# Rope scores of the cached pages as two matmuls on a high-and-low stack, and two weight blocks of the next stage computed at the end of the page stage

## The chip, the cores and the metric

The kernel runs on one core of a Trainium2 chip. Its time is the device time of one execution in microseconds (us). A core has a tensor engine (PE, with its weight loads as PEld), a vector engine (DVE), a scalar engine (ACT), GpSimd (POOL), and a queue that issues most of the DMAs (SP). The engines run their own instruction streams and meet only at semaphores.

## The reference

One layer of a hybrid decoder serves a prompt of 256 tokens and 8 sample sequences of 4 new tokens each (288 token columns in all, T below). Per layer:

```
xn = RMSNorm(x)
h  = x + W_out( sig(g_A) * W_A(mLSTM(xn)) + sig(g_B) * W_B(MLA(xn)) )
y  = h + ConvFFN(RMSNorm(h))
```

The change lies in the MLA branch of the sample sequences. Each has 1024 past positions in 8 pages of 128, chosen by a page table; a page holds 512 latent columns and 64 rotary (rope) columns per position. For each of 16 heads:

```
k      = qk_norm(concat(latent @ w_uk, k_rope))          # 128 + 64 columns
scores = (q . k) * ATTN_SCALE                            # also against the 4 new tokens, masked
p      = softmax(scores)
o      = (p @ latent) @ w_uv
```

The norm of a key is one number for each position and head, so a score is (latent part + rope part) divided by a root. The mLSTM branch takes q, k, v and output gates of 8 heads from one projection of xn.

## The kernel before

All large products are made in a form of float32 called fp32r, for which an operand is split into a high part and the rest: `h*w = hH*wH + hL*wH + hH*wL`, three matmuls that each take one pass. A plain fp32 matmul needs no split; the trace writes it as two records. A transpose is a matmul against `ident`.

The stages follow each other with a barrier between them (`recycle()`):

1. **The queries and prompt attention.** Norm of x; the small projections; queries and keys of 16 heads in a loop `for h in range(BH + 3)`, in which PE makes `keys(h)`, turns chunks of w_uk (`flip`), and makes the absorbed queries (q times w_uk) of the samples. `qrS` is the rope part of the sample queries, 64 x 16 heads x 32 tokens.
2. **The page stage.** For 8 sample sequences (`batch`), 8 pages each: `turn(b, j+1)` transposes the next page (4 transposes of latent columns into PSUM bank 4, one of the 64 rope columns into bank 7), ACT copies the high part into `latH` (`hi`) and DVE subtracts for `latL` (`lo`); then `keys(b, j)` makes 5 groups of columns for the key norms, and in group 0 64 more columns, the scores (16 heads x 4 tokens), by 12 fp32r matmuls a group. The rope part of the scores is one fp32 matmul ahead of them in group 0: `rT` (64 x 128, the page's rope turned) by `qrC` (64 x 64), line 1521. ACT squares the groups (`squares`), DVE sums them (`sums`). The softmax and values of sequence b-1 are spread over the pages of b. Batches 0, 1, 6 and 7 are written out, 2 to 5 are a loop.
3. **The end of the page stage.** For the last sequence nothing is left to put beside: scale, maxima, exps, `values`, `last_denominators`, `turn_out` (line 1606), 128 small matmuls by w_uv (line 1650), four transposes (line 1656), and the store of the result to DRAM (`hb_dram[:, :, S_P:]`). ACT and DVE then split the first weight block (`split_hi`, `split_lo` of `At(N0)`). SP has meanwhile brought back xnH and xnL from DRAM (semaphore `xn_back`); their place in SBUF, and that of the split weights, is that of w_uk in the page stage.
4. **The head stage.** 8 mLSTM heads, 6 weight blocks each. `block(n)` is 48 matmuls: 16 chunks by xnH and xnL with the high weights, then 16 with the low ones. ACT makes `split_hi(n+1)`, DVE `split_lo(n+1)` during block n, in two buffers; SP keeps four 1 MB weight loads in the buffers `stage`. N0 is 9, so the first two blocks of head 0 are At(N0) and At(N0 + 1).
5. Branch and output projections and the FFN, in the same blocks. The branch stage reads back the attention output `hb`.

PE runs in order. Nothing plans the order at run time: it is the order of the text, and a semaphore wait holds back all that is behind it on its engine.

## Time and profile before

| | us |
|---|---|
| median of 3 runs | 2946.97 (2946.59 to 2951.3) |
| the profiled execution's own time | 2953.18 |
| its span, first to last instruction | 2951.4 |
| PE busy (share) | 2896.2 (98%) |
| DVE busy | 1429.4 (48%) |
| ACT busy | 1138.8 (39%) |
| mean granted PE clock | 0.991 |

Busy times overlap between engines. A PE matmul's duration holds its latency, so matmuls that follow each other without a gap overlap in the records; what one costs is the distance from its start to the next one's start. The granted clock is 1.00 at 2.4 GHz and 0.50 at 1.2 GHz.

### The profile page before, as it was taken

How to read it: one execution, taken by the hardware profiler on the slowest of the kernel's cores; microseconds unless marked ns; L12 is line 12 of the kernel's file. 1: busy time of each engine (PE TensorE's matmuls, PEld its weight loads, DVE VectorE, ACT ScalarE, POOL GpSimd, SP SyncE). 2: the span in 40 equal slices, each digit the busy share in tenths (PEclk: the TensorE clock that was granted, in tenths of full speed). 3: DMA queues.
4: the chain of work that ended last, by engine and by line, in shares of the span. 5: the costliest groups of instructions: out<-in, count | busy, mean ns of one | idle time of the engine just before them, and what ended most of it. 6: DMA issues, size and time to landing. Idle time of an engine off the chain costs nothing. (4 is left out here: it accounts for less than half of the span.)

```text
span 2951.4 us, 49867 instructions
## 1 busy us (share of the span) xinstructions
PE 2896.2 (98%) x19398; PEld 2699.2 (91%) x19398; DVE 1429.4 (48%) x2174; ACT 1138.8 (39%) x1875; POOL 104.9 (4%) x346
## 2 busy tenths in 40 slices
PE   8998999999999998999999999999999999999999
PEld 7865898888898896899999999999999999999999
DVE  4465433333333332355555434445667654667644
ACT  5535332332332231344444333334444433444433
POOL 0100000000000000000000000002100000000100
PEclk9998999999999998999999999999999999999999
DMA  6522301001001102756565655556555556555464
GB/s 204 208 80 88 106 1 33 17 17 33 29 5 33 33 1 93 208 157 197 171 186 173 189 171 160 167 151 199 165 163 164 162 148 175 172 170 161 145 180 129
DMA packets 620546, 372.13 MB, mean 126 GB/s; under 512 B 23928, under 2 KB 602050, under 8 KB 619336
## 3 DMA queue, kind: packets, MB, share of 16 engines
q1 hardware_dynamic: 608200, 357.63, 40.6%
q10 hardware_dynamic: 11824, 11.50, 1.1%
q8 instruction: 112, 1.84, 0.2%
q0 software_dynamic: 368, 0.81, 0.1%
q14 instruction: 42, 0.34, 0.0%
HBM read 347.16 MB, written 22.75 MB: 125 GB/s over the span
## 5 line engine op out<-in xcount | busy, mean ns | idle before, releaser
L287 DVE TENSOR_TENSOR w_lo_b<-stage,w_hi_b 128x2048 fp32r<-128x2048 f32 (+1 forms) x289 | 619.2, 2143 | 425.0 <-ACT w_hi_b L280 424.9
L299 PE MATMUL bank<-xnH,w_hi_b 128*128 128x288 f32 x2784 | 756.2, 299 | 6.3 <-PEq L191 6.3
L300 PE MATMUL bank<-xnL,w_hi_b 128*128 128x288 f32 x2784 | 750.9, 296 | 0.0
L280 ACT ACTIVATE w_hi_b<-stage 128x2048 fp32r<-128x2048 f32 (+1 forms) x289 | 517.9, 1792 | 572.4 <-PE bank L304 536.8
L299 PEld LDWEIGHTS bank<-xnH,w_hi_b 128*128 128x128 f32 x2784 | 524.5, 188 | 15.9 <-issue 15.3
L300 PEld LDWEIGHTS bank<-xnL,w_hi_b 128*128 128x128 f32 x2784 | 524.2, 188 | 0.3
L1524 PE MATMUL bank<-ukH,latH 128*128 128x384 f32 (+2 forms) x1280 | 458.0, 358 | 0.0
L1526 PE MATMUL bank<-ukH,latL 128*128 128x384 f32 (+2 forms) x1280 | 452.4, 353 | 0.0
L1525 PE MATMUL bank<-ukL,latH 128*128 128x384 f32 (+2 forms) x1280 | 452.0, 353 | 0.0
L1755 DVE TENSOR_REDUCE rk<-sq_n 128x3 f32<-128x384 f32 (+1 forms) x320 | 184.9, 580 | 508.3 <-ACT sq_n L1679 508.3
L304 PE MATMUL bank<-xnH,w_lo_b 128*128 128x288 f32 x2784 | 396.6, 295 | 0.0
L304 PEld LDWEIGHTS bank<-xnH,w_lo_b 128*128 128x128 f32 x2784 | 378.2, 188 | 0.0
L1679 ACT ACTIVATE sq_n<-bank 128x384 f32<-128x384 f32 (+1 forms) x320 | 163.9, 512 | 443.1 <-PE bank L1526 443.1
L299 PE MATMUL bank<-haH,w_hi_b 128*128 128x288 f32 x1024 | 278.1, 299 | 6.8 <-PEq L191 3.9
L300 PE MATMUL bank<-haL,w_hi_b 128*128 128x288 f32 x1024 | 276.7, 297 | 0.0
L1524 PEld LDWEIGHTS bank<-ukH,latH 128*128 128x128 f32 x1280 | 240.9, 188 | 16.9
L1526 PEld LDWEIGHTS bank<-ukH,latL 128*128 128x128 f32 x1280 | 240.8, 188 | 14.4
L1525 PEld LDWEIGHTS bank<-ukL,latH 128*128 128x128 f32 x1280 | 240.9, 188 | 13.0
L299 PEld LDWEIGHTS bank<-haH,w_hi_b 128*128 128x128 f32 x1024 | 194.1, 190 | 7.5 <-issue 7.3
L300 PEld LDWEIGHTS bank<-haL,w_hi_b 128*128 128x128 f32 x1024 | 194.9, 190 | 0.0
L304 PE MATMUL bank<-haH,w_lo_b 128*128 128x288 f32 x1024 | 151.9, 295 | 0.0
L304 PEld LDWEIGHTS bank<-haH,w_lo_b 128*128 128x128 f32 x1024 | 141.5, 188 | 0.0
(471 smaller groups left out, 2786.1 us busy)
## 6 DMA issues: line engine op xcount, KB each, us to landing
stage<-in_w_in_dram SPq DMA_DIRECT2D x88, 1024.0 KB, 5.0
stage<-in_w_up_dram SPq DMA_DIRECT2D x88, 1024.0 KB, 5.3
stage<-in_w_down_dram SPq DMA_DIRECT2D x64, 704.0 KB, 4.5
latf<-in_cache_kv_latent_dram SPq DMA_DIRECT2D x64, 256.0 KB, 2.5
stage<-in_w_branch_a_dram SPq DMA_DIRECT2D x16, 1024.0 KB, 5.6
stage<-in_w_branch_b_dram SPq DMA_DIRECT2D x16, 1024.0 KB, 5.4
stage<-in_w_out_dram SPq DMA_DIRECT2D x16, 1024.0 KB, 5.6
stage<-in_w_uk_dram SPq DMA_DIRECT2D x8, 1024.0 KB, 5.0
```

What stands on the lines that cost most here:

```text
L280: act.activation(h, a, ACT.Copy).then_inc(w_hi, 1)
L287: dve.tensor_tensor(lo, a, h.bitcast(F32), ALU.subtract).then_inc(w_lo, 1)
L299: pe.matmul(out, hi, xH(k), start=first and k == 0, stop=False)
L300: pe.matmul(out, hi, xL(k), start=False, stop=False)
L304: mm = pe.matmul(out, lo, xH(k), start=False, stop=last and k == kc - 1)
L1524: pe.matmul(out, h, ukH[:, k, cols], start=g > 0 and k == 0, stop=False, skip_group_check=g == 0)
L1525: pe.matmul(out, h, ukL[:, k, cols], start=False, stop=False, skip_group_check=g == 0)
L1526: mm = pe.matmul(out, lo, ukH[:, k, cols], start=False, stop=k == LC - 1, skip_group_check=g == 0)
L1679: act.activation(sq[:, (j + g) % 2, 0:(h1 - h0) * NOPE], part, ACT.Square).then_inc(n_sq, 1)
L1755: dve.tensor_reduce(rk[:, b.mod(2), j, h0:h1], sq[:, (j + g) % 2, 0:(h1 - h0) * NOPE].rearrange("p (h d) -> p h d", d=NOPE), AX.X, ALU.add ...
```

## The change

**Rope part.** The first stage makes from `qrS` two stacks of 128 rows: `qHH` (the high part twice) and `qLZ` (the low part over zeros). For that PE multiplies `qrS` by the identity twice, into the two halves of bank 7 (at h = 5), ACT copies and DVE subtracts (at h = 6), and PE waits for it at h = 7. In the page stage `turn` transposes the page's last 128 columns once more, so that the rope lands on partitions 64 to 127 as well; ACT copies twice, and DVE subtracts the second copy: `rS` holds the high part over the low part. The fp32 matmul goes, and two fp32r matmuls of 64 columns with `rS` as stationary operand come behind the first matmul of group 0. `turn` and `keys` wait for DVE's subtraction (`f_rl`) where they waited for ACT's copy (`f_rt`). The rope of the new tokens (`krrT`) is changed alike. DVE's copy into `qrC` goes.

**Two blocks.** Blocks N0 and N0 + 1 move from the start of the head stage into the end of the page stage: N0 ahead of the last `turn_out`, N0 + 1 ahead of the last four transposes. Their splits move with them, and block N0 + 2 gets its `split_hi` at the end of the stage. The w_uv products go to banks 4 and 7 in place of 0 and 1, the transposes to banks 0 and 3 in place of 2 and 3.

**Placement.** The sample part of the attention output has a DRAM tensor of its own, and `hs` lies in `olat`'s place; the head stage waits for its store before it uses that place again. The branch stage reads `hb` with two DMAs.

```
                 sp.wait_ge(e_oev, 2 * p + 2)
-                sp.dma_start(hb_dram[:, 2 * p:2 * p + 2, 0:S_P], ho[:, p % 2]).then_inc(e_st[p % 2], 16)
+                sp.dma_start(hb_dram[:, 2 * p:2 * p + 2, :], ho[:, p % 2]).then_inc(e_st[p % 2], 16)
...
                     pe.wait_ge(ct_ev, 3)
+                    for a in range(2):
+                        mm = pe.matmul(bank[7][a * ROPE:(a + 1) * ROPE, :], ident[0:ROPE, 0:ROPE],
+                                       qrS[:].rearrange("p h (b s) -> p b h s", b=NB), start=True, stop=True)
+                    mm.then_inc(qd_mm, 1)
+                if h == 7:
+                    pe.wait_ge(qd_lo, 1)
...
                     latent_rows(2)
+                if h == 6:
+                    act.wait_ge(qd_mm, 1)
+                    act.activation(qHH[:].rearrange("p b q -> p (b q)"), bank[7][:], ACT.Copy).then_inc(qd_hi, 1)
...
                     dve.wait_ge(r_ss, 1)
+                if h == 6:
+                    dve.wait_ge(qd_z, 1)
+                    dve.wait_ge(qd_hi, 1)
+                    dve.tensor_tensor(qLZ[0:ROPE].rearrange("p b q -> p (b q)"), bank[7][0:ROPE, :],
+                                      qHH[0:ROPE].rearrange("p b q -> p (b q)").bitcast(F32), ALU.subtract).then_inc(qd_lo, 1)
...
                 need(pe, f_lo, b.of(NPG, j))
-                need(pe, f_rt, b.of(NPG, j))
+                need(pe, f_rl, b.of(NPG, j))
...
                     pe.transpose(bank[4][:, k * P:(k + 1) * P], latf[:, b.mod(2), j, k * P:(k + 1) * P], ident)
+                pe.transpose(bank[7][:, P:2 * P], latf[:, b.mod(2), j, KVL - ROPE:], ident)
...
                 pe.wait_ge(f_lo, b.of(NPG, j + 1))
-                pe.wait_ge(f_rt, b.of(NPG, j + 1))
+                pe.wait_ge(f_rl, b.of(NPG, j + 1))
...
                     out = key_bank(g)[:, 0:c1 - c0]
-                    if g == 0:
-                        pe.matmul(out[:, parts(s)[0]], rT[:, a, :], qrC[:, s, :], start=True, stop=False, skip_group_check=True)
...
                         h, lo = latH[:, a, k * P:(k + 1) * P], latL[:, a, k * P:(k + 1) * P]
-                        pe.matmul(out, h, ukH[:, k, cols], start=g > 0 and k == 0, stop=False, skip_group_check=g == 0)
-                        pe.matmul(out, h, ukL[:, k, cols], start=False, stop=False, skip_group_check=g == 0)
-                        mm = pe.matmul(out, lo, ukH[:, k, cols], start=False, stop=k == LC - 1, skip_group_check=g == 0)
+                        pe.matmul(out, h, ukH[:, k, cols], start=k == 0, stop=False)
+                        if g == 0 and k == 0:
+                            pe.matmul(out[:, parts(s)[0]], rS[:, a, :], qHH[:, bass.ds(b.of(), 1), :], start=False, stop=False)
+                            pe.matmul(out[:, parts(s)[0]], rS[:, a, :], qLZ[:, bass.ds(b.of(), 1), :], start=False, stop=False)
+                        pe.matmul(out, h, ukL[:, k, cols], start=False, stop=False)
+                        mm = pe.matmul(out, lo, ukH[:, k, cols], start=False, stop=k == LC - 1)
...
                     pe.matmul(ps, cnL[:, k, :], qh_, start=False, stop=False)
-                pe.matmul(ps, krrT[:], qrS[:].rearrange("p h (b s) -> p b h s", b=NB), start=False, stop=True).then_inc(f_sn, 1)
+                pe.matmul(ps, krrS[:], qHH[:].rearrange("p b q -> p (b q)"), start=False, stop=False)
+                pe.matmul(ps, krrS[:], qLZ[:].rearrange("p b q -> p (b q)"), start=False, stop=True).then_inc(f_sn, 1)
...
             last_denominators(At(NB - 1))
+
+            def first_block(n):
+                block(pe, At(n), At(n), lambda k: xnH[:, k, :], lambda k: xnL[:, k, :])
+            pe.wait_ge(xn_back, 32)
+            first_block(N0)
...
             pe.wait_ge(uv_in, 16 * LC)
-            pe.wait_ge(n_sq, KG * NPG * NB)
...
                     for g in range(4):
-                        mm = pe.matmul(bank[j // 2][g * N_S:(g + 1) * N_S, j % 2 * P:(j % 2 + 1) * P], olat[:, k, 4 * j + g, :],
+                        mm = pe.matmul(bank[(4, 7)[j // 2]][g * N_S:(g + 1) * N_S, j % 2 * P:(j % 2 + 1) * P], olat[:, k, 4 * j + g, :],
...
                 mm.then_inc(f_uv, 1)
+            first_block(N0 + 1)
...
                 for j in range(2):
-                    tr = pe.transpose(bank[2 + i][:, j * P:(j + 1) * P], ol[:, (2 * i + j) * P:(2 * i + j + 1) * P], ident)
+                    tr = pe.transpose(bank[3 * i][:, j * P:(j + 1) * P], ol[:, (2 * i + j) * P:(2 * i + j + 1) * P], ident)
...
                 act.activation(latH[:, j % 2, :], bank[4][:], ACT.Copy).then_inc(f_hi, 1)
-                act.activation(rT[:, j % 2, :], bank[7][0:ROPE, 0:P], ACT.Copy).then_inc(f_rt, 1)
+                act.activation(rS[0:ROPE, j % 2, :], bank[7][0:ROPE, 0:P], ACT.Copy)
+                act.activation(rS[ROPE:, j % 2, :], bank[7][ROPE:, P:2 * P], ACT.Copy).then_inc(f_rt, 1)
...
             exps(At(NB - 1))
+            split_hi(act, At(N0))
+            split_hi(act, At(N0 + 1))
             act.wait_ge(f_uv, 4)
-            act.activation(ol[:, 2 * P:], bank[1][:, 0:2 * P], ACT.Copy).then_inc(f_hq2, 1)
+            act.activation(ol[:, 2 * P:], bank[7][:, 0:2 * P], ACT.Copy).then_inc(f_hq2, 1)
...
                 act.wait_ge(f_h, i + 1)
-                act.activation(hs[:, 8 * i:8 * i + 8, :].rearrange("p h s -> p (h s)"), bank[2 + i][:, 0:2 * P], ACT.Copy).then_inc(f_hev, 1)
-            split_hi(act, At(N0))
+                act.activation(hs[:, 8 * i:8 * i + 8, :].rearrange("p h s -> p (h s)"), bank[3 * i][:, 0:2 * P], ACT.Copy).then_inc(f_hev, 1)
+            split_hi(act, At(N0 + 2))
...
         def _(dve):
-            dve.memset(krrT[:], 0.0).then_inc(f_zero, 1)
+            dve.memset(krrS[:].bitcast(F32), 0.0).then_inc(f_zero, 1)
...
             dve.wait_ge(f_zero, 2)
+            dve.wait_ge(f_kh, 1)
+            low = krrS[ROPE:, 0:N_S]
+            dve.tensor_tensor(low, bank[6][ROPE:, 0:N_S], low.bitcast(F32), ALU.subtract).then_inc(f_neg, 1)
...
                 dve.tensor_tensor(latL[:, j % 2, :], bank[4][:], latH[:, j % 2, :].bitcast(F32), ALU.subtract).then_inc(f_lo, 1)
+                dve.wait_ge(f_rt, b.of(NPG, j + 1))
+                low = rS[ROPE:, j % 2, :]
+                dve.tensor_tensor(low, bank[7][ROPE:, P:2 * P], low.bitcast(F32), ALU.subtract).then_inc(f_rl, 1)
...
                 s = b.mod(2)
-                dve.tensor_copy(qrC[:, s, :].rearrange("p (h q) -> p h q", q=S_S), qrS[:, :, bass.ds(b.of(S_S), S_S)])
...
             total(At(NB - 1))
+            split_lo(dve, At(N0))
+            split_lo(dve, At(N0 + 1))
...
             dve.wait_ge(f_uv, 2)
-            dve.tensor_copy(ol[:, 0:2 * P], bank[0][:, 0:2 * P]).then_inc(f_hq, 1)
-            split_lo(dve, At(N0))
+            dve.tensor_copy(ol[:, 0:2 * P], bank[4][:, 0:2 * P]).then_inc(f_hq, 1)
...
                 for j in range(steps(h)):
-                    if blocks:
+                    if blocks and not (h.i is None and h.c == 0 and j < 2):
...
                     act.activation(dws[:], bank[5][:, 0:DVE_], ACT.Copy, scale=gws[:, bass.ds(h.of(), 1)]).then_inc(H["ds"], 1)
+                    if h.i is None and h.c == 0:
+                        act.wait_ge(e_st[0], 16 * (BH // 4 + 1))
...
                     if blocks:
-                        split_hi(act, n + (j + 1))
+                        if not (h.i is None and h.c == 0 and j < 2):
+                            split_hi(act, n + (j + 1))
...
                     if blocks:
-                        split_lo(dve, n + (j + 1))
+                        if not (h.i is None and h.c == 0 and j < 1):
+                            split_lo(dve, n + (j + 1))
...
             sp.wait_ge(e_st[s], 16 * (BH // 4 + 1 - s))
-        sp.dma_start(hb[:], hb_dram).then_inc(hb_in, 16)
+        sp.dma_start(hb[:, :, 0:S_P], hb_dram).then_inc(hb_in, 16)
+        sp.dma_start(hb[:, :, S_P:], hbs_dram).then_inc(hb_in, 16)
```

What stands on PE around the rope of one page, before (names: `cst` holds the identity, `krr` is the tensor in which `qrC` lies):

```order
L1526 MATMUL bank<-ukH,latL 128x512
L1498 ISA
L86 REGISTER_ALU
L1502 MATMUL bank<-cst,latf 128x128 x4
L1503 MATMUL bank<-cst,latf 64x128
L86 REGISTER_ALU
L1521 MATMUL bank<-krr,rT 128x64
L1524 MATMUL bank<-ukH,latH 128x448
L1525 MATMUL bank<-ukL,latH 128x448
```

and at a page of the changed kernel:

```order
L1568 MATMUL bank<-cst,mxw 128x64
L86 REGISTER_ALU
L1521 MATMUL bank<-cst,latf 128x128 x4
L1522 MATMUL bank<-cst,latf 128x128
L1523 MATMUL bank<-cst,latf 64x128
L86 REGISTER_ALU
L1542 MATMUL bank<-ukH,latH 128x448
L1544 MATMUL bank<-qHH,rS 128x64
L1545 MATMUL bank<-qLZ,rS 128x64
L1546 MATMUL bank<-ukL,latH 128x448
```

A fifth full transpose comes in, and the rope matmul is replaced by two behind the first of the group.

What stands on PE at the end of the page stage, before:

```order
L1557 MATMUL bank5<-cst,psums 64x1
L1558 MATMUL bank5<-cst,psums 64x1
L1606 MATMUL bank6<-cst,ol_3086 128x64 x4
L1650 MATMUL bank0<-stage,olat 32x128 x32
L1650 MATMUL bank1<-latf,olat 32x128 x32
L1656 MATMUL bank2<-cst,ol_3086 128x128 x2
L1656 MATMUL bank3<-cst,ol_3086 128x128 x2
L1446 UNCONDITIONAL_BRANCH
L2037 UNCONDITIONAL_BRANCH
L299 MATMUL bank1<-xnH,w_hi_b 128x288
```

and in the changed kernel, where block N0 begins:

```order
L1579 MATMUL bank5<-cst,psums 64x1
L1580 MATMUL bank5<-cst,psums 64x1
L300 MATMUL bank1<-xnH,w_hi_b 128x288
L301 MATMUL bank1<-xnL,w_hi_b 128x288
L300 MATMUL bank1<-xnH,w_hi_b 128x288
L301 MATMUL bank1<-xnL,w_hi_b 128x288
L300 MATMUL bank1<-xnH,w_hi_b 128x288
L301 MATMUL bank1<-xnL,w_hi_b 128x288
```

The first block stands ahead of `turn_out`, where in the kernel before two branches (the barrier) lay between.

DVE at the same place, before:

```order
L1799 TENSOR_REDUCE psums<-sc_s 128x64
L1801 TENSOR_TENSOR psums<-psums,sc_s 32x64
L1805 RECIPROCAL rs<-bank5 128x1
L1812 TENSOR_SCALAR ol_3086<-bank6,rs 128x512
L1817 COPY olat<-bank6 128x16x4 x4
L1935 COPY ol_3086<-bank0 128x256
L287 TENSOR_TENSOR w_lo_b<-stage,w_hi_b 128x2048
```

and after:

```order
L1834 TENSOR_REDUCE psums<-sc_s 128x64
L1836 TENSOR_TENSOR psums<-psums,sc_s 32x64
L288 TENSOR_TENSOR w_lo_b<-stage,w_hi_b 128x2048 x2
L1840 RECIPROCAL rs<-bank5 128x1
L1847 TENSOR_SCALAR ol_3096<-bank6,rs 128x512
L1852 COPY olat<-bank6 128x16x4 x4
L1972 COPY ol_3096<-bank4 128x256
```

Two splits stand ahead of the reciprocal; the one at the end is gone.

## Rows read from the trace of the kernel before

**Rows 1.** The page: busy us (share of the span) and instructions.

```profile
PE 2896.2 (98%) x19398; PEld 2699.2 (91%) x19398; DVE 1429.4 (48%) x2174; ACT 1138.8 (39%) x1875; POOL 104.9 (4%) x346
```

**Rows 2.** Busy time by stretch: engines, granted PE clock, DMA share, GB/s.

```profile
1155.00:1188.30 33.30, 17.54 (x166) 10.39 (x165) 10.77 (x24) 6.23 (x11) 0.00 (x0) 0.72 0.55 202
```

**Rows 3.** Timeline of PE at one page: start us, us, instruction, count.

```profile
1086.46 0.60 PE L1502 MATMUL bank<-cst,latf 128*128 128x128 f32 x4
1086.89 0.27 PE L1503 MATMUL bank<-cst,latf 128*64 128x128 f32 x1
1087.09 0.43 PE L1521 MATMUL bank<-krr,rT 64*128 64x64 f32 x2
1087.45 0.47 PE L1524 MATMUL bank<-ukH,latH 128*128 128x448 f32 x1
1087.76 0.36 PE L1525 MATMUL bank<-ukL,latH 128*128 128x448 f32 x1
1087.97 0.36 PE L1526 MATMUL bank<-ukH,latL 128*128 128x448 f32 x1
```

**Rows 4.** Timeline of PE: eight records with full weights and 64 columns.

```profile
1142.11 1.00 PE L1606 MATMUL bank<-cst,ol 128*128 128x64 f32 x8
1143.04 0.43 PE L1521 MATMUL bank<-krr,rT 64*128 64x64 f32 x2
```

**Rows 5.** Timeline of ACT at a page: the copy of the turned rope.

```profile
563.70 0.26 ACT L1666 ACTIVATE rT<-bank 64x128 f32<-64x128 f32 x1
```

**Rows 6.** Timeline of PE in the key loop of the first stage.

```profile
168.36 0.62 PE L745 MATMUL bank<-u_reg,xT_reg 128*32 128x512 f32 x2
169.35 0.66 PE L734 MATMUL bank<-cst,stage 128*128 128x128 f32 x4
201.03 0.65 PE L734 MATMUL bank<-cst,stage 128*128 128x128 f32 x4 [1.27 <-DVE u_reg L1249]
```

**Rows 7.** Timeline of PE at the first two `turn`s; idle before in brackets.

```profile
293.28 1.12 PE L1502 MATMUL bank<-cst,latf 128*128 128x128 f32 x4 [2.31 <-DMA latf<-in_cache_k_rope_dram]
296.26 1.11 PE L1502 MATMUL bank<-cst,latf 128*128 128x128 f32 x4 [1.65 <-DVE latL L1750]
```

**Rows 8.** Timeline of PE from the last denominators into the head stage.

```profile
1172.71 1.63 PE L1606 MATMUL bank<-cst,ol 128*128 128x64 f32 x8 [1.12 <-DVE ol L1812]
1175.14 3.64 PE L1650 MATMUL bank<-stage,olat 128*32 128x128 f32 x64 [0.80 <-DVE olat L1817]
1181.09 1.01 PE L1656 MATMUL bank<-cst,ol 128*128 128x128 f32 x4
1188.34 0.58 PE L299 MATMUL bank<-xnH,w_hi_b 128*128 128x288 f32 x1 [6.25 <-PEq L191]
```

**Rows 9.** Timeline of ACT and DVE in the same stretch.

```profile
1163.54 0.24 ACT L1689 ACTIVATE sc_s<-sc_s 32x64 f32<-32x64 f32 x1
1182.41 1.90 ACT L280 ACTIVATE w_hi_b<-stage 128x2048 fp32r<-128x2048 f32 x1
1184.34 2.29 DVE L287 TENSOR_TENSOR w_lo_b<-stage,w_hi_b 128x2048 fp32r<-128x2048 f32 x1 [5.08 <-ACT w_hi_b L280]
```

**Rows 10.** Busy time by stretch there (columns as in rows 2).

```profile
1167.00:1170.00 3.00, 3.00 (x10) 0.71 (x6) 0.00 (x0) 0.00 (x0) 0.00 (x0) 0.55 0.26 111
1170.00:1172.00 2.00, 1.59 (x8) 0.38 (x6) 0.27 (x2) 0.00 (x0) 0.00 (x0) 1.00 0.00 0
1178.00:1180.00 2.00, 2.00 (x45) 2.00 (x41) 0.43 (x1) 0.00 (x0) 0.00 (x0) 0.51 0.04 8
1180.00:1182.00 2.00, 1.87 (x48) 1.29 (x39) 0.00 (x0) 0.73 (x2) 0.00 (x0) 1.00 0.00 0
```

**Rows 11.** The page: DMA issues, KB each, median us to landing.

```profile
stage<-in_w_in_dram SPq DMA_DIRECT2D x88, 1024.0 KB, 5.0
```

**Rows 12.** Timeline of PE: start of the third weight block, and ten matmuls on.

```profile
1203.56 0.29 PE L299 MATMUL bank<-xnH,w_hi_b 128*128 128x288 f32 x1
1204.88 0.30 PE L299 MATMUL bank<-xnH,w_hi_b 128*128 128x288 f32 x1
```

More of the change, by code:

```diff
@@ L198, in build @@
     xT_dram = nc.dram_tensor("xT_scratch", (P, KC, T), F32, kind="Internal").ap()
-    hb_dram = nc.dram_tensor("hb_scratch", (P, BH, T), F32, kind="Internal").ap()
+    hb_dram = nc.dram_tensor("hb_scratch", (P, BH, S_P), F32, kind="Internal").ap()
+    hbs_dram = nc.dram_tensor("hbs_scratch", (P, BH, N_S), F32, kind="Internal").ap()
     xnH_dram = nc.dram_tensor("xnH_scratch", (P, KC, T), F32, kind="Internal").ap()
@@ L313, in build @@
         c_new = sb(kept, "c_new", [N_S, KVL])
-        qrS = sb(kept, "qrS", [ROPE, BH, N_S])
+        qHH = sb(kept, "qHH", [P, NB, BH * S_S], F32R)
+        qLZ = sb(kept, "qLZ", [P, NB, BH * S_S], F32R)
         qlat = sb(kept, "qlat", [P, LC, NB, 2, BH, S_S], F32R)
@@ L424, in build @@
             u_reg = arena("u_reg", [P, 2, 2, KVL], 2 * XB + WB)
+            qrS = arena("qrS", [ROPE, BH, N_S], 2 * XB + WB + 8192)
             smr = arena("smr", [P, BH, N_S], 2 * XB + WB + 10240)
@@ L492, in build @@
             v_mm, v_ev = sem("vv_mm"), sem("vv_ev")
+            qd_mm, qd_z, qd_hi, qd_lo = (sem("qd_" + x) for x in ("mm", "z", "hi", "lo"))
             e_s, e_sc, e_sm, e_mx, e_ex, e_rc, e_nm, e_t, e_tev, e_o, e_oev = (
@@ L1141, in _ @@
                     dve.memset(cnL[:].bitcast(F32), 0.0).then_inc(cn_z, 1)
+                    dve.memset(qLZ[:].rearrange("p b q -> p (b q)").bitcast(F32), 0.0).then_inc(qd_z, 1)
                     dve.wait_ge(x_rt, 1)
@@ L1368, in build @@
             sq = sb(ph, "sq_n", [P, 2, GC])
-            qrC = krr2[0:ROPE, 0:2, 1, :]
-            rT = sb(ph, "rT", [ROPE, 2, P])
+            rS = sb(ph, "rS", [P, 2, P], F32R)
+            mxp = sb(ph, "mxp", [P, 2, P])
+            mxw = sb(ph, "mxw", [HQ, 2, P])
             sqr = sb(ph, "sqr_n", [P, 2, ROPE])
@@ L1379, in build @@
             sc = sb(ph, "sc_s", [P, 2, NJ, HQ])
-            mxp = sb(ph, "mxp", [P, 2, P])
             mxc = sb(ph, "mxc", [HQ, 2])
-            mxw = sb(ph, "mxw", [HQ, 2, P])
             psums = sb(ph, "psums", [P, 2, HQ])
@@ L1386, in build @@
             olat = sb(ph, "olat", [P, LC, BH, N_S])
-            hs = sc[:].rearrange("p a j q -> p (a j q)")[:, 0:BH * N_S].rearrange("p (h s) -> p h s", h=BH)
-            krrT = sb(ph, "krrT", [ROPE, P])
+            hs = olat[:].rearrange("p k h s -> p (k h s)")[:, 800:800 + BH * N_S].rearrange("p (h s) -> p h s", h=BH)
+            krrS = sb(ph, "krrS", [P, P], F32R)
             gb = sb(ph, "gb", [P, 2 * AH])
@@ L1409, in build @@
             n_k, n_sq, n_red = (sem("n_" + x) for x in ("k", "sq", "red"))
+            f_kh, f_rl = sem("f_kh"), sem("f_rl")
             (f_kt, f_fold, f_neg, f_zero, f_sn, f_sn1, f_scn, f_t, f_hi, f_rt, f_lo, f_ra, f_rr, f_rc, f_sev, f_snc, f_m8, f_mxp,
@@ L1491, in _ @@
                     sp.wait_ge(f_hev, 2)
-                    sp.dma_start(hb_dram[:, :, S_P:], hs).then_inc(e_st[0], 16)
+                    sp.dma_start(hbs_dram, hs).then_inc(e_st[0], 16)
                 @blk.tensor
@@ L1629, in batch @@
                                 gates(j)
-                    pe.transpose(bank[6][0:ROPE, 0:N_S], krr[0:N_S, 2, :], ident[0:N_S, 0:N_S]).then_inc(f_kt, 1)
+                    pe.transpose(bank[6][:, 0:N_S], krr2[0:N_S, 2].rearrange("p a e -> p (a e)"), ident[0:N_S, 0:N_S]).then_inc(f_kt, 1)
                     pe.wait_ge(f_neg, 1)
@@ L1721, in _ @@
                     act.wait_ge(f_zero, 2)
-                    act.activation(krrT[:, 0:N_S], bank[6][0:ROPE, 0:N_S], ACT.Copy).then_inc(f_neg, 1)
+                    act.activation(krrS[:, 0:N_S], bank[6][:, 0:N_S], ACT.Copy).then_inc(f_kh, 1)
                     for g in range(4):
@@ L2379, in _ @@
                         if j == i:
-                            act.wait_ge(hb_in, 16)
+                            act.wait_ge(hb_in, 32)
                             act.activation(hbH[:, q0:q1, :], hb[:, q0:q1, :], ACT.Copy).then_inc(hb_h, 1)
```

## Prediction, made blind

> **What bounds the kernel now.** I read the page first: PE is busy for 98% of the span [rows 1], so time is won only where PE does less, or where it stands still or runs at the lower clock. The table by stretch shows where that is: from the end of the last page to the head stage PE is busy for 17.54 us of 33.3, at a mean granted clock of 0.72 [rows 2]. The page stage itself is dense. The timeline gives the cost of one page's rope [rows 3], and the timeline of PE, ACT and DVE at the end of the stage gives the chain there [rows 8, 9]. Durations come from the profiled execution, 2953.18 us, 6.21 above the median of 2946.97; I work out a difference and take it from the median.
>
> **The page loop.** From the first transpose to the second large matmul a page takes 1087.76 - 1086.46 = 1.30 us [rows 3]: 0.43 for four transposes (0.107 each), 0.20 for the narrow one (0.107 and the time until the next matmul may begin), 0.36 for the two records of the fp32 rope matmul, 0.31 for the first large matmul, whose weight load nothing hides; the next takes 0.21. The change takes out the 0.36. It adds one transpose, 0.107. The narrow transpose is still the last, so its 0.20 and the 0.31 stay.
>
> The two fp32r matmuls of 64 columns load full weights each, and no record before has just this form. The nearest is `turn_out`: eight records with 128 x 128 weights and 64 columns take 1143.04 - 1142.11 = 0.93 us, 0.116 each [rows 4]; they are fp32, but a record of 64 columns streams for far less, so the weight load sets the distance. I take this: 0.23 for the pair. The cheap end is the stream alone: a matmul of 448 columns takes 0.21 [rows 3], so 64 columns take 0.03, 0.06 the pair. The dear end is the record of the rope matmul itself, 0.18 [rows 3], with a weight load of 0.11 laid bare behind them: 0.47. So a page goes from 1.30 to 0.54 + 0.20 + 0.31 + 0.23 = 1.28; 64 pages give 1.3 us. By the ends it would be 12 us gained (0.36 - 0.107 - 0.06 = 0.19 a page) or 14 us lost (0.22 a page).
>
> The Trainium skill ("TensorE: Matmul & The Clock Gate", section "LDWEIGHTS (loading the stationary operand)") gives columns / 1.2 ns for a weight load, so 107 ns for 128; the 0.116 above agrees. The same page, section "Back-to-back issue gap", puts a matmul of up to 64 columns at about 25 ns where nothing else holds it; by that alone the pair would cost 0.05 us, and the kernel would end where the second rival has it.
>
> ACT makes one more copy a page, 0.26 us [rows 5], and DVE a subtraction of 64 x 128, which I put at as much. Both stand behind `hi` and `lo` of the next page, more than 10 us ahead of its use, on engines that are busy for 39 and 48% [rows 1]; queued behind them are the squares and sums of group 0, whose PSUM bank PE wants back only a page later. Cost: nothing; without that cover it would be 0.5 us a page. Only at the first two pages does PE wait for this chain: the second `turn` waited 1.65 us for `latL` [rows 7], and now waits for the rope's subtraction behind it, +0.25 us. The new tokens' rope gets a DVE step ahead of their scores, 0.3 us; they are followed by a wait of 2.31 us for the page's DMA [rows 7], which hides it.
>
> **The first stage.** PE gets two fp32 matmuls of 64 x 64 weights and 512 columns into two halves of a bank. The nearest are the four column-tiled ones of line 745, which run side by side: from 168.36 to 169.35, 0.99 us for all four [rows 6]. The halves do not share columns of the array either, so I take 1.0; two in turn would be 2.0; the low end is 0, since PE later stands for 1.27 us for DVE [rows 6] and might only get there later. PE's wait at h = 7 I put at nothing: two key products and two sets of transposes lie between the multiplication and it, against one ACT copy and one DVE subtraction. Both are queued ahead of copies that PE waits for two steps later; if they slip, it is by the 0.7 us or so of a DVE operation of 512 columns, within the ends. DVE's zeroing of `qLZ` lies in the wait for x at the start.
>
> **The end of the page stage.** Before: PE is done with the denominators at 1172.71 - 1.12 = 1171.59, waits, `turn_out` at 1172.71, 0.80 of waiting, w_uv from 1175.14, transposes at 1181.09, and then nothing for 6.25 us, since ACT and DVE split block N0 until 1184.34 + 2.29 = 1186.63 before the barrier; PE resumes at 1188.34, 1.7 later [rows 8, 9]. The third block begins at 1203.56. Block length: ten matmuls take 1.32, so 48 take 6.3 [rows 12]; the first two took 15.2, 2.6 more than 12.6, because the clock had fallen.
>
> After, step by step:
> - Operands of block N0 are there: ACT is free at 1163.78, its two splits (1.90 each) end at 1167.6, DVE's (2.29 each) at 1170.4; xnH and xnL have landed when DMA falls still before 1170 [rows 9, 10]. Slack of DVE 1.2 us: its reciprocal is behind the splits.
> - Block N0 from 1171.6 to 1177.9. The clock had risen from 0.55 to 1.00 by 1170, after PE had been busy for some 6 us, and was at 0.51 again by 1178 [rows 10]; now PE does not pause behind 1171.6.
> - `turn_out` 0.93 [rows 4] to 1178.8; wait for `olat` 0.8 [rows 8], 1179.6.
> - w_uv: at clock 0.51 45 matmuls took 2.00 us; at 1.00 44 took 1.09 (1180.00 to 1181.09, the other 4 of the 48 being the transposes) [rows 8, 10]. 128 by 0.025 are 3.2, to 1182.8, where before they took 5.95.
> - Block N0 + 1 to 1189.1. From the first transpose to the end of ACT's copies took 1182.41 - 1181.09 = 1.3 [rows 8, 9]: 1190.4. SP's two weight loads start behind w_uv, at 1182.8; at 5.0 us [rows 11] the first is there by 1188.
> - `split_hi` of N0 + 2, 1.9: 1192.3; the barrier 1.7: block N0 + 2 begins at 1194.0. DVE's `split_lo` follows at once (its memsets and 2.3 us, about 3.5) and is wanted after 32 matmuls, over 4 us on.
>
> 1203.56 - 1194.0 = 9.5 us earlier, but an idle time of about 4 us lets the clock fall as the 6.25 did before, so block N0 + 2 pays the 2.6. Gain 6.9 us. What was late before, two splits and a barrier, is now one high split and the barrier; the next in line, loads of blocks N0 + 4 and on, have two blocks (12 us) from their issue against 5.0 each.
>
> The store and reload of `hb` I put at nothing: both are issued by SP, and the reload's first user is ACT two blocks later, 12.6 us. If the short pieces of the sample part held up the loads behind it on the queue by more than the three blocks that are loaded ahead, PE would stand; at worst a few us.
>
> **Sum.** -6.9 - 1.3 + 1.0 + 0.25 = -6.9 us: 2953.2 becomes 2946.3 in a profile, the median 2946.97 becomes 2940.1. A measurement of this kernel tells 0.2% (5.9 us) from no change, so the forecast is faster by slightly more than that.
>
> **Rivals.**
> 1. *The clock falls in the middle of the end stage.* For it: before, w_uv ran at 0.51 until 1180 although PE had stood for only 1.12 and 0.80 us since it was last at 1.00 [rows 8, 10]. Against: a dense block of 6.3 us now precedes. Price: w_uv back to 5.95 (+2.8) and a further 2.6 in block N0 + 1, 5.4 in all: 2945.5.
> 2. *The small matmuls hide their weight loads.* The pair at 0.06: 0.17 a page better, 10.9 us: 2929.2. Against it speak the 0.116 of rows 4, though those are fp32.
> 3. *The other side: the pair stalls the large matmuls.* Both add into columns that the matmul just ahead is still writing, and the large one behind finds its weights not loaded: 0.47 for the pair, 0.24 a page more than taken, 15.4 us: 2955.5. It makes the kernel no faster from a pair cost of 0.23 + 6.9 / 64 = 0.34, and slower by 0.2% from 0.43. For it: every change of shape in rows 3 costs 0.1. Against: `rS` is a full 128 x 128 operand, as are its neighbours.
> 4. *The moved blocks do not fill the gap.* If ACT's or DVE's splits or the reload of xn come after 1171.6 by several us, `turn_out` is held behind block N0 and the gap only moves: 2947, no change. The slack of 1.2 us speaks against it.
>
> **How the numbers follow.** Forecast 0.53, rivals in order 0.17, 0.12, 0.08, 0.10. The forecast's own spread, 2936 to 2943, comes from the first stage's 0 to 2 us, a tenth of a microsecond a page more or less in part, and the run-to-run spread of before. Faster than 2941.1: rival 2, and 0.65 of the forecast: 0.46. Slower than 2952.9: rival 3 and a rest: 0.09. The same: 0.45. The range leaves out the far part of rivals 2 and 3: 2931 to 2948.
>
> **What the profile after would show.** A page's stretch from first transpose to the second large matmul (L1546) at 1.28 us, L1544 to L1546 0.23 apart; PE idle of about 4 us, no more 6.25, ahead of the third block; w_uv in 3 to 4 us; clock 1.00 from 1170 to about 1190; the last stretch from the last denominators to block N0 + 2 of 22 us where it was 32. The forecast is wrong if the pair is not near 0.23, if block N0 has a wait ahead of it, or if the head stage runs dry of weights.

## The result, and the profile after

The changed kernel takes 2929.63 us (median of 4 runs, 2927.95 to 2931.32) against 2947.57 (4 runs) for the kernel before, measured beside it: ratio 0.9936, 95% interval [0.9924, 0.9947], 17.9 us less. The forecast was 2940.1, the range 2931 to 2948; the time lies below it. The profiled execution took 2930.21 us with a span of 2928.4, so in the profiles the difference is 23.0 us of span.

One execution of the kernel before beside e1 to e4 (7029.46 us) and one of e3 (5666.08 us) were slow, and the medians below leave them out.

The page of the kernel after answers to [rows 1] with less PE time (21.4 us less) from slightly more instructions:

```profile
PE 2874.8 (98%) x19466; PEld 2696.7 (92%) x19466; DVE 1453.3 (50%) x2233; ACT 1157.6 (40%) x1940; POOL 108.2 (4%) x346
```

The timeline of PE at a plain page after (start us, us, instruction, count), beside [rows 3]:

```profile
1036.83 0.60 PE L1521 MATMUL bank<-cst,latf 128*128 128x128 f32 x4
1037.27 0.27 PE L1522 MATMUL bank<-cst,latf 128*128 128x128 f32 x1
1037.37 0.27 PE L1523 MATMUL bank<-cst,latf 128*64 128x128 f32 x1
1037.40 0.45 PE L1542 MATMUL bank<-ukH,latH 128*128 128x448 f32 x1
1037.69 0.19 PE L1544 MATMUL bank<-qHH,rS 128*128 128x64 f32 x1
1037.71 0.28 PE L1545 MATMUL bank<-qLZ,rS 128*128 128x64 f32 x1
1037.83 0.45 PE L1546 MATMUL bank<-ukL,latH 128*128 128x448 f32 x1
1038.11 0.36 PE L1547 MATMUL bank<-ukH,latL 128*128 128x448 f32 x1
```

From the first transpose to the third large matmul this is 1038.11 - 1036.83 = 1.28 us; in [rows 3] it is 1087.97 - 1086.46 = 1.51. 64 pages by 0.23 are 14.7. The page loop, from its first large matmul to the end of its last, took 857.0 us before (298.13 to 1155.17) and 843.2 after (298.79 to 1141.95): 13.9 less, where the forecast had 1.3.

The timeline of PE from the last denominators into the head stage after (in brackets: idle before, and what ended it), beside [rows 8]:

```profile
1156.96 0.40 PE L300 MATMUL bank<-xnH,w_hi_b 128*128 128x288 f32 x1
1165.22 1.96 PE L1676 MATMUL bank<-stage,olat 128*32 128x128 f32 x64 [0.80 <-DVE olat L1852]
...
1179.45 0.37 PE L300 MATMUL bank<-xnH,w_hi_b 128*128 128x288 f32 x1 [3.50 <-PEq L191]
```

Block N0 begins right behind the denominators, at 1156.96, block N0 + 2 at 1179.45, 22.5 us later. The busy time by stretch (duration, PE, PEld, DVE, ACT, POOL busy, granted PE clock, DMA share, GB/s), a stretch of 33.3 us from just ahead of block N0, against 17.54 us busy at 0.72 in [rows 2]:

```profile
1155.00:1188.30 33.30, 29.00 (x312) 26.91 (x309) 9.08 (x15) 6.06 (x10) 0.63 (x1) 1.00 0.43 134
```

The 23.0 us of span by stretch: up to the first large matmul +0.7; the page loop -13.9; from its end to the end of the third weight block -10.8 (55.0 before, 44.1 after); the rest +1.0. In that rest ACT waits 4.41 us for a weight load (until 1191.09), and PE's fifth block begins 7.1 us behind its fourth, where 6.4 is usual: 0.7 us in which the head stage did run dry of weights, once.

### The profile page after: what moved, and what is told of

Read it like the earlier page. It is cut to its first block and busy times, and to the rows that moved or that the text cites. A ratio compares the mean times of both kernels' runs of the same rounds, so it can differ in the third digit from the quotient of the medians.

```text
span 2928.4 us, 50135 instructions
## 1 busy us (share of the span) xinstructions
PE 2874.8 (98%) x19466; PEld 2696.7 (92%) x19466; DVE 1453.3 (50%) x2233; ACT 1157.6 (40%) x1940; POOL 108.2 (4%) x346
## 5 line engine op out<-in xcount | busy, mean ns | idle before, releaser
L300 PEld LDWEIGHTS bank<-xnH,w_hi_b 128*128 128x128 f32 x2784 | 523.0, 188 | 14.2 <-issue 12.8
L1546 PE MATMUL bank<-ukL,latH 128*128 128x384 f32 (+2 forms) x1280 | 458.0, 358 | 0.0
L1542 PEld LDWEIGHTS bank<-ukH,latH 128*128 128x128 f32 x1280 | 241.2, 188 | 12.8
L1546 PEld LDWEIGHTS bank<-ukL,latH 128*128 128x128 f32 x1280 | 241.0, 188 | 12.4
```

Source lines behind the costliest of these rows:

```text
L300: pe.matmul(out, hi, xH(k), start=first and k == 0, stop=False)
L1542: pe.matmul(out, h, ukH[:, k, cols], start=k == 0, stop=False)
L1546: pe.matmul(out, h, ukL[:, k, cols], start=False, stop=False)
```

## Experiments

Theory A, formed from the traces of before and after: the 0.20 us behind the narrow transpose [rows 3] was not that transpose's. It was a wait of the weight load behind it, because the rope matmul's weights have 64 rows and its neighbours' 128. Rival B: the plain fp32 type of the rope matmul made it. Rival C: the narrow transpose made it, and in the changed kernel something hides it. The timelines of PE's weight loads, before:

```profile
1086.78 0.11 PEld L1503 LDWEIGHTS bank<-cst,latf 128*64 128x64 f32 x1
1087.09 0.29 PEld L1521 LDWEIGHTS bank<-krr,rT 64*128 64x128 f32 x2 [0.20 <-issue]
1087.45 0.19 PEld L1524 LDWEIGHTS bank<-ukH,latH 128*128 128x128 f32 x1
```

and after:

```profile
1037.27 0.11 PEld L1523 LDWEIGHTS bank<-cst,latf 128*64 128x64 f32 x1
1037.38 0.19 PEld L1542 LDWEIGHTS bank<-ukH,latH 128*128 128x128 f32 x1
1037.49 0.19 PEld L1544 LDWEIGHTS bank<-qHH,rS 128*128 128x128 f32 x1
```

Behind the narrow transpose's load the next one stood 0.31 us away before, and 0.11 after. Beside e1 to e4 the kernel before took 2948.63 us, beside e5 to e8 2946.84, and beside e9 to e12 2947.09; each ratio is against the one beside it.

**e1: the rope part alone.** The changed kernel with both blocks, their splits and the split of N0 + 2 back in the head turn:

```
-                    pe.wait_ge(xn_back, 32)
-                    first_block(N0)
...
-                    first_block(N0 + 1)
...
-                            if blocks and not (h.i is None and h.c == 0 and j < 2):
+                            if blocks:
```

> The changed kernel with its two weight blocks put back at the start of the head stage; rope stack and placement stay. Theory A (the 64-row fp32 matmul made PE wait 0.20 us a page for its own weight load, and that wait went with it): the page loop keeps its whole gain of 13.9 us, the start costs 0.7, so 13 us faster than before (ratio about 0.9955). Rival (the page gain depended on the blocks, or was one profile's chance): 3 us or less, as I predicted at first.

Measured: 2937.53 us against 2948.63, ratio 0.9963 [0.995, 0.9976], 11.1 us less. Its page loop takes 842.7 us, close to the 843.2 after.

**e2: the blocks alone.** The kernel before with both blocks moved as in the change.

> The kernel before with only the two weight blocks moved into the end of the page stage. Theory: the end stage gives 7 to 10 us in a profile: 6.9 by the shorter chain, 2.6 more if the clock stays at 1.00 through the idle time of 3.5 us ahead of block N0 + 2. Against the median of before, whose profile was a slow one at this place, 5 to 7 us faster (ratio about 0.998). The page loop must stay at 857.0 us. Rival (the two parts help each other): the parts alone add up to clearly less than the 18 us of both.

Measured: 2943.44, ratio 0.9981 [0.9972, 0.999], 5.2 us less; its page loop takes 856.1 us (857.0 before). 0.9963 by 0.9981 is 0.9944, and both together gave 0.9936: the parts add. So about three fifths of the gain came from the part that I had put at 1.3 us.

**e3: the old rope matmul over 128 rows.** The kernel before; its fp32 matmul and its narrow transpose stay, but `rT` has 128 rows, the lower 64 zero (the other operand's lower rows hold whatever finite numbers lie there):

```
-            qrC = krr2[0:ROPE, 0:2, 1, :]
-            rT = sb(ph, "rT", [ROPE, 2, P])
+            qrC = krr2[:, 0:2, 1, :]
+            rT = sb(ph, "rT", [P, 2, P])
...
+                    dve.memset(rT[ROPE:], 0.0)
```

> The kernel before with the fp32 rope matmul made over 128 rows, the lower 64 of its weights being zeros: same type, same columns, same place. Theory A (PE waits when the rows of the weights change from 128 to 64 and back): the 0.20 us ahead of the rope's weight load and the like behind it go, 0.15 to 0.25 us a page, 10 to 16 us in all (ratio about 0.996). Rival B (it is the fp32 type behind the transposes that waits, whatever the rows): no change, page stretch 1.51 us as before. Rival C (the narrow transpose ahead makes the next matmul wait): no change either.

Measured: 2929.89, ratio 0.9938 [0.9925, 0.9951], 18.7 us below the kernel before: as much as the whole change, with not one operation fewer. Timeline of PE at a plain page of e3:

```profile
1027.85 0.60 PE L1502 MATMUL bank<-cst,latf 128*128 128x128 f32 x4
1028.28 0.27 PE L1503 MATMUL bank<-cst,latf 128*64 128x128 f32 x1
1028.39 0.33 PE L1521 MATMUL bank<-krr,rT 128*128 128x64 f32 x2
1028.53 0.45 PE L1524 MATMUL bank<-ukH,latH 128*128 128x448 f32 x1
...
1029.03 0.36 PE L1526 MATMUL bank<-ukH,latL 128*128 128x448 f32 x1
```

The stretch is 1.18 for 1.51. The weight loads of that page tell where the 0.33 went:

```profile
1028.17 0.11 PEld L1503 LDWEIGHTS bank<-cst,latf 128*64 128x64 f32 x1
1028.28 0.30 PEld L1521 LDWEIGHTS bank<-krr,rT 128*128 128x128 f32 x2
1028.50 0.19 PEld L1524 LDWEIGHTS bank<-ukH,latH 128*128 128x128 f32 x1
```

From the narrow transpose's load to the rope's it is 0.11 for 0.31, so the whole 0.20 of the wait is gone; from the rope's load to that of the first large matmul 0.22 for 0.36, another 0.14. By the starts of the matmuls the same 0.33 falls otherwise, 0.11 for 0.20 ahead of the rope matmul, 0.14 for 0.36 behind it and 0.50 for 0.52 in the rest, since the rope matmul starts together with its load before and 0.11 behind it here. Its loop takes 835.3 us, 21.7 less. Type and narrow transpose are as before, so B and C fall. The size is above the 0.15 to 0.25 that I expected: the way back to 128 rows costs 0.14 on top of the 0.20.

**e4: the kernel before, profiled again,** without an edit, to see what two profiles of one kernel differ by.

> The kernel before, profiled once more. If the profile of before was slow at the end of the page stage by the clock's timing (values of the last sequence 7.48 us there, 5.2 in the changed kernel), this one may show another share of it: 5 to 7.5 us for the same 18 records. The page loop is 857.0 us again within 0.5.

Its loop takes 856.9 us (857.0). A loop's length is still not good to that in general, and the reason is its first page. Across all profiles the time from the loop's first large matmul to the second page's first transpose is 12.3 to 14.2 us, and PE is at the lower clock for 1.7 to 5.3 us of it, longest where the page is longest (e6) and shortest where it is shortest (e10). The busy time by stretch shows one place in it before and then in e9 (columns as above, the clock is third from the end):

```profile
300.00:302.00 2.00, 2.00 (x6) 1.78 (x6) 2.00 (x2) 0.12 (x1) 0.00 (x0) 0.50 0.67 194
300.00:302.00 2.00, 2.00 (x11) 1.86 (x11) 2.00 (x1) 0.52 (x4) 0.00 (x0) 1.00 0.50 154
```

From the second page on, the loop takes 843.4 us in both profiles of the kernel before and 843.5 in e2, 829.1 after and 828.7 in e1, 822.7 in e3. There e3 gains 20.7 us, 0.33 for each of 63 pages, and the change 14.3, or 0.23 each.

The sixteen `values` records of the last sequence, behind several us of idle time, differ more from profile to profile: 6.47 us here, 6.55 in the first profile, 5.87 in e2, 5.21 after. (What I expected above set two different things side by side: with the two records of the new tokens the eighteen took 6.20 after, not 5.2.)

**e5: 64 rows in the new format.** The changed kernel with one matmul over 64 rows for the pair (it leaves out the low parts of the rope term):

```
-pe.matmul(out[:, parts(s)[0]], rS[:, a, :], qHH[:, ...], ...)
-pe.matmul(out[:, parts(s)[0]], rS[:, a, :], qLZ[:, ...], ...)
+pe.matmul(out[:, parts(s)[0]], rS[0:ROPE, a, :], qHH[0:ROPE, ...], ...)
```

> The changed kernel with the pair of small matmuls over 128 rows of weights replaced by one small matmul over 64 rows, same number format; it leaves out the low parts of the rope term. Theory A (each change of the weights between 128 and 64 rows makes PE wait, whatever the format): one small matmul of 0.11 us less a page, but the wait of 0.20 ahead and some 0.1 behind is back, in all +0.1 to +0.2 a page, 64 pages: 2936 to 2943 us. Rival B (the wait of before came from the 32-bit format of its rope matmul, or from the narrow output of the transpose ahead of it): 0.11 a page less, 2922 to 2923 us.

Measured: 2943.48, ratio 0.9986 [0.9977, 0.9995]: with one matmul fewer a page it is 13.9 us slower than the changed kernel. Timeline of its weight loads at a page:

```profile
1046.90 0.19 PEld L1542 LDWEIGHTS bank<-ukH,latH 128*128 128x128 f32 x1
1047.31 0.18 PEld L1544 LDWEIGHTS bank<-qHH,rS 64*128 64x128 f32 x1 [0.22 <-issue]
1047.53 0.19 PEld L1545 LDWEIGHTS bank<-ukL,latH 128*128 128x128 f32 x1
```

and of PE:

```profile
1046.36 0.60 PE L1521 MATMUL bank<-cst,latf 128*128 128x128 f32 x4
...
1047.31 0.29 PE L1544 MATMUL bank<-qHH,rS 64*128 64x64 f32 x1
...
1047.84 0.36 PE L1546 MATMUL bank<-ukH,latL 128*128 128x448 f32 x1
```

The load of the 64 rows comes 0.41 us behind the one ahead of it, where the same load with 128 rows comes 0.11 behind (1037.38 to 1037.49 after): it isn't begun under the large matmul. The page's stretch is 1047.84 - 1046.36 = 1.48, 0.20 more than after; 64 by 0.20 are 12.8. One load of 0.11 is gone as well, so the 64 rows cost some 0.31 here, near e3's 0.33. The format is fp32r and the wide transpose is there, so the rows alone bring the wait back. Theory A holds from both sides.

**e6: the rope twice, one transpose.** The changed kernel; GpSimd writes the rope columns side by side, so that one full transpose makes the stack, and ACT copies once:

```
-                        pe.transpose(bank[7][:, P:2 * P], latf[:, b.mod(2), j, KVL - ROPE:], ident)
-                        pe.transpose(bank[7][0:ROPE, 0:P], latf[:, b.mod(2), j, KVL:], ident).then_inc(f_t, 1)
+                        pe.wait_ge(f_d, b.of(NPG, j + 1))
+                        pe.transpose(bank[7][:, 0:P], dup[:, j % 2]..., ident).then_inc(f_t, 1)
...
+    rope = latf[:, b.mod(2), j, KVL:].unsqueeze(1).broadcast_to([P, 2, ROPE])
+    pool.tensor_tensor(dup[:, j % 2], rope, ones..., ALU.mult).then_inc(f_d, 1)
```

> The changed kernel with the rope columns written twice side by side by GpSimd (an operation of 128x128 a page, beside all else), so that one full transpose gives the stack that the changed kernel gets from a wide and a narrow one, and one ACT copy in place of two. Theory A has nothing against it: one weight load and transpose of 0.11 us less a page, 7 us: 2922 to 2924 us. Rival: GpSimd slows VectorE's page work or is late with the first page of a turn: 2928 to 2935 us.

Measured: 2923.18, ratio 0.9913 [0.9898, 0.9928], 6.5 us below the changed kernel; the loop takes 836.9 us for 843.2, 0.10 a page, the weight load of the transpose that went.

**e7: the small fix and the blocks.** e3 and e2 in one kernel.

> The kernel before with both things that the runs so far found to pay, each in its smallest form: the 32-bit rope matmul over 128 rows with zeros below (18.3 us alone) and the two blocks in the end stage (5.6 alone). If the two add as the parts of the change do: 2947.5 - 23.9 = 2923 to 2925 us, faster than the changed kernel. Rival: the changed kernel's remaining gain is shared by both, 2928 to 2930.

Measured: 2923.07, ratio 0.9911 [0.9896, 0.9926]. They add (0.9938 by 0.9981 is 0.9919). The high-and-low stacks, the first stage's products and the extra transpose are not needed for the gain.

**e8: only block N0 moved.** The changed kernel with block N0 + 1 back in the head turn.

> The changed kernel with only the first of the two blocks in the end stage; the second is back in the head turn. If the idle ahead of the head turn (3.5 us in the changed kernel, 6.3 before) comes back and the clock falls after it as before (2.6 us): 2929.6 + 3 + 2.6 = 2935 us. If the idle comes back and the clock stays: 2932 to 2933. If the first block alone fills what there was to fill: 2929 to 2930.

Measured: 2932.54, ratio 0.9948 [0.9934, 0.9961], 2.9 us above the changed kernel; the intervals overlap. The timeline of PE at the start of its head stage:

```profile
1173.54 0.58 PE L300 MATMUL bank<-xnH,w_hi_b 128*128 128x288 f32 x1 [5.90 <-PEq L191]
1173.91 0.45 PE L301 MATMUL bank<-xnL,w_hi_b 128*128 128x288 f32 x1
1174.15 0.45 PE L300 MATMUL bank<-xnH,w_hi_b 128*128 128x288 f32 x1
```

The long idle time is back and the matmuls behind it stand 0.24 apart, against 0.13 at the full clock. From the end of the loop to the end of the third block this profile takes 50.5 us against 44.1. Of the 6.4 between them 0.9 is the `values`, 2.4 the longer idle time, and 2.8 the block behind it at the lower clock (9.4 us for 6.6). The last of these the changed kernel's profile was spared, but profiles like it were not, as the part on the clock below shows. So the second block is worth some 3 us by the medians, though the intervals do not settle it.

**e9: the other matmuls of fewer rows.** The kernel before with its rope matmul untouched; the spread of the maxima (64 rows) and the values of the new tokens (32 rows) are filled up to 128 with zeros:

```
-            mxw = sb(ph, "mxw", [HQ, 2, P])
+            mxw = sb(ph, "mxw", [P, 2, P])
...
-                            n = P if j < NPG else N_S
+                            n = P
```

> The kernel before, its rope matmul untouched, with the two other matmuls of a turn whose weights have fewer than 128 rows filled up with zeros to 128: the spread of the maxima (64 rows) and the values of the new tokens (32 rows). Theory A (the change of rows costs, wherever it stands): the weight loads around the spread stand 0.54 and 0.36 us apart in the trace of before where 0.23 and 0.22 are usual, 0.45 a turn, and the two values matmuls take 0.99 where two of their neighbours take 0.47, 0.52 a turn; 7 or 8 turns: 7 us less, 2939 to 2941 us. Rival (a page's wait belongs to the small rope matmul and its place, not to the rows): no difference, 2946 to 2948 us.

Measured: 2943.02 against 2947.09, ratio 0.9983 [0.9974, 0.9992]; the loop takes 852.5 us, 4.5 less. Timeline of PE at the spread, before:

```profile
428.55 0.39 PE L1526 MATMUL bank<-ukH,latL 128*128 128x512 f32 x1
428.87 0.43 PE L1546 MATMUL bank<-cst,mxw 64*128 64x64 f32 x2
429.23 0.66 PE L1502 MATMUL bank<-cst,latf 128*128 128x128 f32 x4
```

and in e9:

```profile
427.31 0.39 PE L1526 MATMUL bank<-ukH,latL 128*128 128x512 f32 x1
427.55 0.33 PE L1546 MATMUL bank<-cst,mxw 128*128 128x64 f32 x2
427.71 0.61 PE L1502 MATMUL bank<-cst,latf 128*128 128x128 f32 x4
```

From the large matmul to the transposes 0.68 us before and 0.40 here: the rule holds in another place. With the values I was wrong. In the timelines of PE, before:

```profile
482.04 1.94 PE L1601 MATMUL bank<-latf,sc_s 128*64 128x512 f32 x8
483.91 1.07 PE L1601 MATMUL bank<-c_new,sc_s 32*64 32x512 f32 x2
484.90 0.66 PE L1502 MATMUL bank<-cst,latf 128*128 128x128 f32 x4
```

and in e9:

```profile
480.45 1.94 PE L1601 MATMUL bank<-latf,sc_s 128*64 128x512 f32 x8
482.21 1.02 PE L1601 MATMUL bank<-c_new,sc_s 128*64 128x512 f32 x2
483.17 0.66 PE L1502 MATMUL bank<-cst,latf 128*128 128x128 f32 x4
```

The two records still take 0.96 us (0.99), so their length has nothing to do with rows, and of my 0.52 a turn only 0.14 over the whole stretch (2.86 to 2.72) was there. A cause that fits, but that no run tests: the other eight alternate between two halves of the columns and run side by side, and the last one has no partner. Of the loop's 4.5 us, 0.28 + 0.14 for 7 turns explain 2.9, and 0.06 a turn ahead of the narrow transpose 0.4 more. The remaining 1.2 is not the edit's: it is the first page, 12.4 us here for 13.6 at a clock that rose earlier (e4), and from the second page on the loop takes 840.1 us, 3.3 less than before.

**e10 and e11: all of it.** e7 and e6, each with e9's edit.

> The rope matmul over 128 rows, the two blocks in the end stage (2923.1 us together) and the two other matmuls of a turn over 128 rows. If the parts add: 7 us less, 2915 to 2918 us. Rival: 2922 to 2924 us, the turn's matmuls give nothing.

> The changed kernel with the doubled rope columns (2923.2 us) and the two other matmuls of a turn over 128 rows. If the parts add: 2915 to 2918 us, within 2 us of the version with the 32-bit rope matmul, since a page costs both 1.24 us from the first transpose to the third large matmul. Rival: 2922 to 2924 us.

Measured: e10 2918.29, ratio 0.9906 [0.9891, 0.9921]; e11 2920.99, ratio 0.9913 [0.99, 0.9927]. Their loops take 831.5 and 832.8 us, 4.1 and 4.0 less than e7's and e6's (3.4 and 3.2 from the second page on), so the edit adds in the loop. In the medians e10 is 4.8 below e7 and e11 2.2 below e6, inside the intervals. e10 is the fastest that computes everything: 28.8 us below the kernel before, measured beside it, and 11 below the changed kernel.

**e12: without the rope matmul.** The kernel before; its page scores lack the rope part, transposes and copies stay.

> The kernel before without the rope matmul of the page scores (it leaves out that part of the scores). A page has 1.57 us from the first transpose to the third large matmul, 1.24 with the rope matmul over 128 rows. Theory A: what is left of the rope matmul at 128 rows is its two weight loads, 0.14 us; without it 1.10 a page, 0.47 less than before, 30 us: 2916 to 2919 us. Rival: some of the 0.33 belongs to the stretch itself and stays: 2925 us or more.

Measured: 2915.52, ratio 0.9896 [0.9881, 0.9911], 31.6 us less. The page's stretch from first transpose to third large matmul, in the timeline of PE:

```profile
1028.28 0.60 PE L1502 MATMUL bank<-cst,latf 128*128 128x128 f32 x4
1028.71 0.27 PE L1503 MATMUL bank<-cst,latf 128*64 128x128 f32 x1
1028.74 0.45 PE L1522 MATMUL bank<-ukH,latH 128*128 128x448 f32 x1
1029.23 0.37 PE L1524 MATMUL bank<-ukH,latL 128*128 128x448 f32 x1
```

0.95 us, 0.56 less than in [rows 3], and 0.23 less than e3. The narrow transpose is there with no wait behind it, 0.03 us by the matmuls. So the rope matmul of before cost 0.56 us a page: 0.23 for itself and 0.33 for its 64 rows, while its two records are 0.36 apart from the next [rows 3]. I had expected 0.47 and an end at 2916 to 2919; at 128 rows it costs 0.23, not the 0.14 of its two loads.

**The clock in the end stage.** The first matmul of the head stage, e7:

```profile
1171.31 0.58 PE L299 MATMUL bank<-xnH,w_hi_b 128*128 128x288 f32 x1 [3.48 <-PEq L191]
```

Its idle time is that of the changed kernel, but three us from there were granted 0.55 (busy time by stretch of e7, columns as above):

```profile
1171.40:1174.40 3.00, 3.00 (x14) 3.00 (x15) 2.89 (x4) 2.39 (x4) 0.63 (x1) 0.55 0.34 73
```

and of the changed kernel in its place:

```profile
1179.45:1182.45 3.00, 3.00 (x22) 3.00 (x23) 2.80 (x4) 2.50 (x4) 0.63 (x1) 1.00 0.16 47
```

In e6 PE started its block at the full clock, and the clock fell in the middle of it, between 1 and 2 us in:

```profile
1172.19:1175.19 3.00, 3.00 (x15) 3.00 (x14) 3.00 (x2) 0.50 (x1) 0.00 (x0) 0.53 0.82 185
```

Over all profiles: behind 5.85 to 6.51 us of idle time the clock had fallen in seven of seven (before, e4, e1, e3, e8, e9, e12). Behind 3.48 to 3.53 it was down when PE resumed in five (e2, e5, e7, e10, e11) and fell within the block in e6; only in the profile of the changed kernel did it stay at 1.00. The block took 6.6 us there and 7.9 to 9.3 in the other six.

## Why the prediction was wrong, point by point

- **The page loop: the step that failed** is "The narrow transpose is still the last, so its 0.20 and the 0.31 stay." The 0.31 stayed (0.29). The 0.20 did not: between narrow transpose and large matmul there is 0.03, and between their weight loads 0.11 where it was 0.31. I had booked an idle time to the instruction ahead of it; it belonged to the one behind, whose weights have 64 rows (e3, e5, e12). By the working, the stretch to the third large matmul should have been 1.28 + 0.21 = 1.49; it is 1.28. Of the 0.21, 0.20 are this step. It makes 64 x 0.20 = 12.8 us, as much as the loop fell beyond the forecast (13.9 for 1.3). Between the forecast and the result lie 10.5, less than that, and most of the difference is that the blocks gave 1.7 less in the medians than I had put (e2), which is within the intervals. The Trainium skill has a rule that I had not weighed: its page "TensorEngine Tiling (Array Packing)", section "Key Properties", says that a change of the tiling mode drains TensorE. It does not say whether a plain matmul with fewer rows or columns of weights is such a change. The runs behave that way for rows, with 0.33 us for there and back; for columns they show no such cost (0.03 to the next matmul in e12).
- **The pair** I put at 0.23. From the first large matmul to the third it is 0.71 (1037.40 to 1038.11), against 0.49 in e12, which has no rope matmul: 0.22, two weight loads of 0.11. So this term was right, and the nearest row, `turn_out` [rows 4], was the one to take. The sign that I had named for it was not: L1544 to L1546 are 0.14 apart and the stretch to L1546 is 1.00, since the other 0.08 of the pair's cost shows only behind L1546, which stands 0.29 ahead of the next where e12 has 0.20. The section "LDWEIGHTS (loading the stationary operand)" of the Trainium skill's page "TensorE: Matmul & The Clock Gate" gives columns / 1.2 ns, so 107 ns for 128, and the loads agree (0.11). The 25 ns of its section "Back-to-back issue gap", which that section gives without a weight load, did not decide here.
- **Rival 2 named the right time for the wrong reason.** Its 2929.2 is the measured time, but the pair costs 0.22, not 0.06. By luck the 0.17 a page that it took off the pair is near the 0.20 that the forecast had too much in another term. A hit on the number would have taught a false rule; the rows tell them apart.
- **Rival 3**, the other side, named a change of shape as a cost; it is one, but on the kernel before, and the change takes it away. `rS` is full, as I wrote against the rival, and I did not ask the same of `rT`.
- **The end stage** by its steps was right: 22.4 us from the denominators to block N0 + 2, 22.5 measured; idle about 4, measured 3.50. The penalty of 2.6 for the clock was not paid in the profiled run of the changed kernel; in the six other profiles with that idle time 1.2 to 2.7 us were. (With blocks 6.4 apart at the full clock, not 6.3, the 2.6 is 2.4.) The blocks alone gave 5.2 us (e2) for 6.9 forecast. So rival 1 did not come, nor rival 4: block N0 has no wait ahead of it.
- **The profile overstates the end stage**: 10.8 us there. The `values` were 1.3 us shorter in it and the clock stayed up, both of which vary between profiles of like kernels (e4, e7).
- **The first stage** I put at +1.0. The loop begins 0.7 us later in the profile after, but in e1, with the same first stage, 1.4 earlier than before, so no run tells this term from the spread of profiles. The second `turn` waits 2.06 us for DVE's subtraction, `rS`, where it waited 1.65 for `latL`: +0.41 for +0.25, too small to matter.
- **The range** was too narrow for its own working. The page term rested on four distances of 0.1 to 0.3 us, each times 64; 0.20 off in one of them left it. My dear and cheap ends concerned the new instructions alone, none an interval that I took over as unchanged.

## What to carry to other kernels

Before a removed instruction is priced, look at the idle time on both sides of it, and ask of each neighbouring interval which of its two ends it belongs to; an experiment that alters only one end settles it. Where small matmuls with 64 rows of weights stand among ones with 128, fill them up with zeros first: here that took two buffers and a memset, and gave as much as a rewrite of the rope term and a moved pair of blocks. And a number that comes out as a rival said isn't yet that rival's mechanism.

## What the runs showed of the hardware

- A change of the weights from 128 to 64 rows and back costs PE 0.33 us in this kernel (e3 against before, by the weight loads: 0.20 ahead, 0.14 behind), and in e5 0.41 us pass between two loads that stand 0.11 apart at 128 rows. It holds in fp32 and in fp32r. A change in the columns (128 x 64 among 128 x 128, the narrow transpose) costs nothing to see: 0.03 to the next matmul in e12, and loads 0.11 apart in the profile after. Weights of 32 rows behind ones of 64 columns showed 0.14 a turn at most (e9).
- A transpose of 128 columns costs its weight load, 0.10 to 0.11, in the page (e6 against the changed kernel).
- Two small matmuls of 64 columns with full weights cost their two weight loads, 0.22 (after against e12).
- An idle time of 3.5 us does not settle the clock behind it: 1.00 throughout in one profile, the lower level at once in five, and in one a fall between 1 and 2 us into the block. Likewise the loop's first page, with 1.7 to 5.3 us at the lower clock, took 12.3 to 14.2 us.
